# One core, a hybrid decoder block: keys replicated by transfers, output products halved, query rotation on GpSimd, and a re-ordered attention and tail

## What is computed

```python
xn = rms_norm(x, norm1_g)
u, q, k, v, qi, ki, wi, gs, ga = split(xn @ w_in)          # q, k, qi, ki get a rotary embedding
y_ssm = s5_mixer(u, ...)                                   # 32 groups of 64 complex states, a scan over the tokens
#   y = einsum(xr, c_re) - einsum(xi, c_im) + d * u ; gelu ; y * sigmoid(y @ w_glu + b_glu)
s = einsum('bthd,bsd->bths', qi, ki) * ID ** -0.5          # 16 index heads
score = einsum('bths,bth->bts', relu(s), wi)               # causal; the 64 best keys of each token are kept
p = softmax(q . k over the kept keys); y_att = p @ v       # 8 heads, 2 key heads
x = x + (sigmoid(gs) * (y_ssm @ w_proj_ssm) + sigmoid(ga) * (y_att @ w_proj_attn)) @ w_out
h = rms_norm(x, norm2_g)
gates = softmax over the 4 best of 32 of (h @ w_router)
for e in range(32):                                        # w_moe_in[e]: 1024 x 2048, w_moe_out[e]: 1024 x 1024
    z = h @ w_moe_in[e] + b_moe_in[e]
    out += gates[:, e] * (clamped_swiglu(z) @ w_moe_out[e] + b_moe_out[e])
return rms_norm(x + out, norm_f_g)
```

## Time and profile before

| | |
|---|---|
| Median of 3 runs | 1170.8 us (1169.01 to 1173.03) |
| The profiled execution | 1169.42 us, of which the span from first to last instruction is 1167.6 us |
| TensorE busy | 1118.3 us (96%) |
| VectorE busy | 343.2 us (29%) |
| ScalarE busy | 157.2 us (13%) |
| GpSimd busy | 0.7 us, seven memsets |
| Moved by DMA | 437.01 MB, mean 374 GB/s |

### The profile page before, as it was taken

One profiled execution on the slowest core, in us unless ns is written; L12 is line 12 of the kernel. 1 busy time (PEld: TensorE's weight loads), 2 busy tenths in 40 slices (PEclk: granted clock), 3 DMA queues, 4 the chain that ended last, 5 costly groups with the idle time before them and its releaser, 6 DMA issues.

```text
span 1167.6 us, 13800 instructions
## 1 busy us (share of the span) xinstructions
PE 1118.3 (96%) x5578; PEld 490.3 (42%) x5578; DVE 343.2 (29%) x760; ACT 157.2 (13%) x331; POOL 0.7 (0%) x7
## 2 busy tenths in 40 slices
PE   9999998989999999999999999999999999999995
PEld 8877786843333333333333333333333333333332
DVE  7999774221112221111111112211111111111112
ACT  2311433130001100010000001000000000000002
POOL 0000000000000000000000000000000000000000
PEclk9999998999999999999999999999999999999999
DMA  8343665589999999999999999999999999999992
GB/s 334 145 145 109 266 261 216 217 321 430 427 427 428 430 428 428 429 428 428 429 429 428 428 430 429 427 429 429 428 428 429 429 427 429 429 429 427 428 429 105
DMA packets 33434, 437.01 MB, mean 374 GB/s; under 512 B 3840, under 2 KB 3968, under 8 KB 5504
## 3 DMA queue, kind: packets, MB, share of 16 engines
q1 hardware_dynamic: 33120, 435.96, 89.1%
q10 hardware_dynamic: 288, 0.69, 0.2%
HBM read 435.58 MB, written 1.05 MB: 374 GB/s over the span
## 4 chain that ended last, share of the span: by engine, by line
PE 63%; DMA 22%; SPq 7%; DVE 6%; issue 1%; ACT 1%; DVEq 0%
PE ps L1277 25%; DMA mem<-in_w_moe 21%; PE ps L1325 13%; PE ps L1010 7%; SPq L359 7%; PE ps L1236 4%; PE ps L1253 3%; DVE mem L574 3%; PE ps L1211 2%; PE ps L1288 2%; PE ps L1188 1%; PE ps L1244 1%; PE ps L1310 1%; PE ps L1056 1%; PE ps L1107 1%
## 5 line engine op out<-in xcount | busy, mean ns | idle before, releaser
L1277 PE MATMUL ps<-mem,late 128*64 128x512 f32 x2048 | 458.2, 595 | 22.9 <-DMA mem<-in_w_moe 22.7
L1277 PEld LDWEIGHTS ps<-mem,late 128*64 128x64 f32 x2048 | 141.6, 137 | 330.7 <-issue 282.3
L1325 PE MATMUL ps<-mem,late 128*64 128x512 f32 x1024 | 226.8, 595 | 0.0
L938 DVE TENSOR_SCALAR late<-ps 128x512 f32<-128x512 f32 x32 | 22.1, 692 | 689.0 <-PE ps L1277 689.0
L1010 PE MATMUL ps<-mem 128*128 128x256 f32 x640 | 143.4, 382 | 0.0
L1010 PEld LDWEIGHTS ps<-mem 128*128 128x128 f32 x640 | 119.9, 190 | 21.0 <-issue 4.5
L1325 PEld LDWEIGHTS ps<-mem,late 128*64 128x64 f32 x1024 | 70.7, 137 | 133.3 <-issue 128.1
L537 ACT ACTIVATE late<-late 128x512 f32<-128x512 f32 x32 | 20.2, 630 | 514.9 <-DVE late L938 514.9
L1253 PE MATMUL ps<-late 64*128 64x512 f32 x256 | 63.6, 615 | 0.8 <-ACT late L544 0.8
L1236 PE MATMUL ps<-xs,late 128*64 128x512 f32 x256 | 63.5, 618 | 0.8 <-DVE late L574 0.8
L574 DVE TENSOR_TENSOR mem<-mem 128x1024 f32<-128x1024 f32 (+8 forms) x89 | 61.2, 729 | 6.5 <-ACT mem L429 3.7
(11 more groups left out here) (161 smaller groups left out, 518.9 us busy)
## 6 DMA issues: line engine op xcount, KB each, us to landing
mem<-in_w_moe SPq DMA_DIRECT2D x192, 2048.0 KB, 42.4
mem<-in_w_mix SPq DMA_DIRECT2D x26, 1024.0 KB, 5.4
mem<-in_w_mix SPq DMA_DIRECT2D x2, 512.0 KB, 7.3
out<-xs SPq DMA_DIRECT2D x2, 512.0 KB, 3.1
late<-in_turn_w SPq DMA_DIRECT2D x1, 640.0 KB, 3.9
late<-in_mix_tables SPq DMA_DIRECT2D x1, 576.0 KB, 14.8
mem<-in_x_t ACTq DMA_DIRECT2D x1, 512.0 KB, 4.6
mem<-in_x_t SPq DMA_DIRECT2D x1, 512.0 KB, 5.8
```

The source lines that it names most:

```text
L938: ve.tensor_scalar(gate_z, z[:, 0], LIMIT, None, ALU.min).then_inc(z_gate, 1)
L1277: i = pe.matmul(ps[r, n // 2, :], h_sel[:, k % 4, k // 4, :], w[:, 512 * n:512 * n + 512], start=(k == 0), stop=(k == KD - 1))
L1325: i = pe.matmul(ps[64 * q:64 * q + SLOTS, 2, :], act_tile(k), w[:, 512 * q:512 * q + 512], start=(k == 0), stop=(k == KF - 1))
```

## The change

1. **Output products.** VectorE subtracts and adds the four products in pairs, so that `y_out` has two products and two coefficient blocks (8 matmuls instead of 16).
2. **Query rotation.** The two `rope(qi_t)` go from VectorE to GpSimd, which starts as soon as QI0 and QI1 have been copied out.
3. **Keys by transfers.** The jobs KR0 to KR2 and their evictions go; SP copies the rotated keys with twelve transfers of 32 partitions.
4. **Order in the mixer stage.** The score jobs stand one x_job later (from the end of S3 to A1), `logits(0)` stands before A2 and `logits(1)` right after it, ahead of GLU; VectorE makes `y_raw` after `scores`; the choice for tile 1 is split; mask, exponentials, probabilities and attention of tile 1 run in two halves of four heads; `project` starts with the first half.
5. **Residual and bias.** The residual no longer goes through `diag`: the raw values are kept in `raw` and opened into the four banks by four matmuls with the identity (`open_sums`) in the routing stretch. The output bias goes into expert 1 as four matmuls on four row groups. Expert part 5 is issued after `opened` and `x_norm`, since `raw` lies there.
6. **The end.** `flag` is read in the second expert instead of after the last; ScalarE loads the Sqrt table before the end; the last norm goes tile by tile.

The diff, cut to its core:

```diff
-                for n, c in enumerate((0, 2, 1, 1)):
+                for n in range(2):
                     for a in range(4):
                         ins = pe.matmul(ps[32 * a:32 * a + 32, 2 + i // 2, (i % 2) * T:(i % 2) * T + T],
-                                        c_t[c][:, i, 32 * a:32 * a + 32], prod_out[n][:, a, :],
-                                        start=(n == 0), stop=(n == 3))
+                                        c_t[n][:, i, 32 * a:32 * a + 32], prod_out[2 * n][:, a, :],
+                                        start=(n == 0), stop=(n == 1))
...
-                tt(ct[2], tv[1], tv[0], ALU.subtract)
...
-                tt(prod_out[3], state_re, ei, ALU.mult).then_inc(out_ok, 1)
+                link(tt(prod_out[3], state_re, ei, ALU.mult))
+                tt(prod_out[0], prod_out[0], prod_out[1], ALU.subtract)
+                tt(prod_out[2], prod_out[2], prod_out[3], ALU.add).then_inc(out_ok, 1)
...
+            gp.wait_ge(consts_in, 16)
+            for n in range(2):
+                part = qi_t[:, 2 * n:2 * n + 2]
+                gp.wait_ge(*evicted(f"QI{2 * n}"))
+                gp.wait_ge(*evicted(f"QI{2 * n + 1}"))
+                if n:
+                    gp.wait_ge(queries_roped, 1)
+                gp.tensor_tensor(rope_c, part, cb, ALU.mult)
+                gp.tensor_tensor(rope_s, part, sn, ALU.mult).then_inc(rope_parts, 1)
+                gp.wait_ge(rope_parts, n + 1)
+                gp.tensor_tensor(part[:, :, 0, :], rope_c[:, :, 0, :], rope_s[:, :, 1, :], ALU.subtract)
+                gp.tensor_tensor(part[:, :, 1, :], rope_c[:, :, 1, :], rope_s[:, :, 0, :], ALU.add).then_inc(
+                    queries_roped, 1)
...
+            sp.wait_ge(roped, 1)
+            for n in (2, 0, 1):
+                for a in range(4):
+                    sp.dma_start(krep[32 * a:32 * a + 32, n], kk[32 * n:32 * n + 32]).then_inc(krep_in[n], 16)
+            load("A2")
...
-            x_job("S3", between=score_job)
-            x_job("A0", between=lambda step: score_job(4 + step))
+            x_job("S3", between=scores_from(-3))
+            x_job("A0", between=scores_from(1))
             y_out(3)
-            x_job("A1")
-            pe.wait_ge(tables_in, 16)
+            x_job("A1", between=scores_from(5))
+            logits(0)
             x_job("A2")
-            logits(0)
+            logits(1)
...
-            x_job("A3")
-            logits(1)
+            pe.wait_ge(tables_in, 16)
+            turn_prob(0)
+            x_job("A3")
...
-            sp.wait_ge(rstd_ok, 1)
+            sp.wait_ge(opened, 1)
+            sp.wait_ge(x_norm, TT)
             load_first(5)
...
-                        if adds:
-                            pe.wait_ge(diag_ok, 1)
...
-                body(first + 1, pairs, 1, opens=isinstance(c, int))
+                body(first + 1, pairs, 1, out_bias=isinstance(c, int))
+                if most_tokens:
+                    most_tokens()
```

More of the change, by code:

```diff
@@ L457, in _ @@
                 gate("S", gate_s, V_BG, n)
-            for n in range(3):
-                evict(f"KR{n}", krep[:, n], pair)
             def relus(*jobs):
@@ L542, in body @@
                                   ACT.Copy).then_inc(act_t_ok, 1)
+                    if tail:
+                        ready(ACT.Sqrt)
                     ac.wait_ge(chunk_used, j * NT + NT)
@@ L767, in scores, with choose_keys @@
                 ve.wait_ge(v_chain, chain[0])
-            def choose_keys(t):
+            def choose_keys(t, first, end):
                 w = P * (t + 1)
-                link(tt(score[:, t, 0:w], score[:, t, 0:w], causal[:, t, 0:w], ALU.add))
-                src = score[:, t, 0:w]
+                if first == 0:
+                    link(tt(score[:, t, 0:w], score[:, t, 0:w], causal[:, t, 0:w], ALU.add))
                 dst = taken[:, t, 0:w]
-                for n in range(NSEL // 8):
+                for n in range(first, end):
+                    src = dst if n else score[:, t, 0:w]
@@ L807, in _ @@
+            i.then_inc(y_raw_ok, 1)
+            choose_keys(0, 0, NSEL // 8)
+            mask(0, 0, NH)
+            choose_keys(1, 0, 5)
+            probabilities(0, 1, 0, NH)
+            choose_keys(1, 5, NSEL // 8)
             ve.wait_ge(*evicted("GLU1"))
@@ L809, in _ @@
             tt(y_ssm, y_gelu, glu_g, ALU.mult).then_inc(y_ssm_ok, 1)
-            choose_keys(1)
-            probabilities(0)
-            ve.wait_ge(*evicted("PS1"))
-            ve.wait_ge(*evicted("PS0"))
-            tt(p_ssm[:, 0:4, :], p_ssm[:, 0:4, :], gate_s[:, 0:4, :], ALU.mult)
-            mask(1)
+            for n in range(2):
+                mask(1, 4 * n, 4 * n + 4)
+            for n in range(2):
+                probabilities(1, 2 + n, 4 * n, 4 * n + 4)
             ve.wait_ge(rout_in, 16)
@@ L1085, in _ @@
             x_job("S2")
-            pe.wait_ge(roped, 1)
-            for n in range(3):
-                b = job(f"KR{n}")
-                r = slice(32 * n, 32 * n + 32)
-                for half in range(2):
-                    i = pe.matmul(b[:, half * T:half * T + T], sel[r, :], kk[r, half, :], start=True, stop=True)
-                i.then_inc(rot_done, 1)
             def score_job(n):
@@ L1216, in _, with open_sums @@
             aux(KD - 1)
+            def open_sums(t, q):
+                pe.wait_ge(tok_ok, 4 * q + 4)
+                return pe.matmul(ps[:, 4 + 2 * t + q, :], ident, raw[:, t, 512 * q:512 * q + 512], start=True,
+                                 stop=False, skip_group_check=True)
+            open_sums(0, 0)
+            open_sums(1, 0)
+            open_sums(0, 1)
             pe.wait_ge(picked_ok, 1)
@@ L1471, in packed_biases @@
     rows[:, 0:512] = b_in.reshape(NE, 4, 512).transpose(1, 0, 2).reshape(P, 512)
-    rows[0:2 * NE, 512:1024] = b_out.reshape(NE, 2, 512).transpose(1, 0, 2).reshape(2 * NE, 512)
+    rows[:, 512:1024] = np.tile(b_out.reshape(NE, 2, 512).transpose(1, 0, 2).reshape(2 * NE, 512), (2, 1))
     return rows
```

302 lines of the change are left out of this document (164 added, 138 removed).

## The result

The changed kernel took **1175.1 us** (median of 5 runs, 1173.74 to 1176.68), against 1170.8. The ratio is 1.0039, with a 95% interval of 1.0021 to 1.0058. So the kernel became slower by 4.3 us (the medians) to 4.6 us (the ratio), little more than the 3.5 us that can be told from no change. The prediction was 1173, in a range of 1162.5 to 1178. The profiled execution took 1175.11 us with a span of 1173.3 us; both are 5.7 us more than those of the profiled one of before.

The account below looks back on a forecast made before the run. Mixer stage and tail were taken to count in full around a weight-paced expert stream. The profiled 1169.4 - 6.7 (all but GpSimd) + 8.7 (GpSimd) = 1171.4, plus 1.4 to the median: 1172.8, say 1173 us; range 1162.5 to 1178.

Parts of the forecast that it names:

- the forecast's side: GpSimd and VectorE take turns at two-input work: delay 5.5 to 11.9 us, time 1169 to 1177, chance 0.47.
- the free case: Rival: GpSimd doesn't slow VectorE, whose operations of 1024 columns stay 1.16 us; 1164 us (1162 to 1167), chance 0.37.
- the held one: Rival: VectorE waits out each of GpSimd's eight operations in the mixer stage; 1177 to 1180 us, chance 0.12.
- What bounds the kernel: Whole run: mixer stage and tail count in full; between them 180 weight parts stream at 4.9 us each.
- Output products: Mixer stage: VectorE's added pairs make TensorE's third `y_out` wait some 4.5 us and start at 105.4, +5.1 us.
- Key transfers: Mixer stage: twelve transfers cost nothing, and the dropped key jobs save TensorE 2.9 us.
- Clock: TensorE: every idle stretch over 3.5 us costs a further 1.6 us through a slower granted clock.
- New order: Mixer stage: `logits(1)` waits 4.8 us plus 1.6 of slow clock, other waits go; W starts at 212.1, +1.5 us.
- routing: End of mixer stage: `open_sums` fill idle time and keep the clock up, `gates_turned` waits; -1.6 + 0.7 = -0.9 us.
- Tail: Experts 30 and 31: 7.8 us of matmuls go, transfers limit this to -5.9; `flag` read -1.0, norm -0.4.
- GpSimd beside VectorE: Mixer stage, rounds 1 and 2: GpSimd's query rotation delays VectorE, bounds 0 to 15.8 us, taken as +8.7.
- GpSimd holds VectorE whole: Rival: each of eight operations is waited out; first `y_out` waits over 14 us, third 17; 1177 to 1180, chance 0.12.

Follow-up runs that it names:

- the first experiment: The changed kernel without GpSimd's eight rotation operations, which only give their signals, so the index queries stay unrotated: 1163.53 us, ratio 0.9934.
- the experiment on the tail alone: The kernel before the change, without the diagonal matmuls of expert 30 and the output-bias matmuls of expert 31: 1164.02 us, ratio 0.9947.
- halves: The changed kernel with the query rotation cut into sixteen GpSimd instructions of half the length: 1174.72 us, ratio 1.0051.

## Why the prediction was right

The time lay in the range, on the forecast's side, and about 2 us above the point. That it lay in the range says little, since 1162.5 to 1178 took in most of the free case and the start of the held one. What was right is the account of the mixer stage, the stream and the tail; the term for GpSimd was too small, and its mechanism was nearer to the rival's. Step by step:

- **What bounds the kernel.** Right. The mixer stage counts in full (+13.4 at W, +12.1 at the first streamed transfer, +12.7 at the last part), the stream takes 4.9 us a part, and the tail counts.
- **Output products.** Right: +5.1 without GpSimd (third `y_out` at 105.4 in the first experiment). The wait before it was 3.45 us for the some 4.5 worked out, because TensorE came later itself after a slow clock behind the first `y_out`; in the kernel with the rotation under the PSUM reads, which had no slow clock there, it was 4.51. In the changed kernel it came at 118.0, not at 114.
- **Key transfers.** Right to cost them at nothing; they landed in 2.0 us each, and the worked-out start of W came out within 0.6 us in the kernel without GpSimd's work (212.7 for 212.1). The key jobs were not put back by themselves, so their -2.9 was measured only within that sum.
- **Clock.** Right in kind, but no fixed price fits. `logits(1)` took 3.57 us after an idle 4.50 us, and 2.01 us without one (the kernels with the copy-outs ahead), so 1.56 for the 1.6 taken. Other runs paid more behind the same wait: 2.6 us with the rotation back on VectorE (3.80 us, and 7.99 instead of 7.17 for the GLU jobs behind it). At the third `y_out` the 1.6 taken for an idle 4.5 us was 3.0 in the first experiment. And the bound of 3.5 us of idle time, below which no price was put, doesn't separate the cases: see the list at the end.
- **New order.** The wait before `logits(1)` was 4.50 (4.8 worked out). Mixer stage up to W +2.1 without GpSimd (+1.5); routing -1.3 (-0.9). Several scattered clock prices stand in this +2.1, so its nearness is partly luck.
- **Tail.** -5.8, and in the experiment on the tail alone -6.0 (-5.9). The `flag` read gave -0.4, inside its bounds of 0 to -2.3 but not the -1.0 taken. Norm -0.7 (-0.4).
- **GpSimd beside VectorE.** This is the term that was mis-sized. The sum took 8.7 us; VectorE was delayed by 12.6, beyond the 5.5 to 11.9 that bounded it, and the time rose by 11.1 to 11.6. Three choices in it were wrong. GpSimd's own time was taken as the middle of 7.3 and 15.8, and undisturbed it is 14.6; that the trace adds up to 15.8 just as the memsets gave is chance, since it includes GpSimd's own waiting. It was put at 54 us and started at 46.4, when QI0 and QI1 had been copied out. And the exemption of a quarter for PSUM reads didn't apply, since no such read of VectorE falls into the two bursts; there stand scans and short operations, nearly all with two inputs in SBUF. So VectorE lost 12.6 of 14.6 us, 0.86, and not three quarters. The sign that was named for the forecast, longer two-input operations of 1024 columns, didn't come: the six after the second burst take 7.03 us with and without GpSimd's work. It was shorter instructions that were held. The estimate by the pages of the Trainium skill, 13.8 us nearly all of it VectorE's delay, was nearer than the sum.

The rival "GpSimd holds VectorE whole" named the true mechanism, each of the eight instructions waited out, with a chance of 0.12 against the forecast's 0.47. It bounded the delay from below at 13 us, just above what came, and its price of 1177 was 2 us too high. The forecast and this rival differ little in kind: VectorE does get a turn after each GpSimd instruction, but only for one short instruction. In one sign both were wrong: the third `y_out` didn't wait 17 us, since TensorE had been held for 15.7 us at the first one already and waited 2.45 at the third.

With 12.6 in place of 8.7 the prediction's own sum for the profiled execution is 1175.3 us, and it took 1175.11. That this fits so closely is luck: between the profiled spans the rotation cost 11.1 us, and the rest of the change gave 5.4 and not 6.7.

The point from which the change is slower was given as a delay of 10.2 us, for slower by over 0.3%. With 12.6 the change is slower by 0.39%, and the interval of the ratio (1.0021 to 1.0058) reaches to both sides of that bound.

## What to carry to other kernels

Moving two-input work from VectorE to GpSimd is no relief while VectorE itself reads two inputs from SBUF: it costs VectorE nearly GpSimd's whole time, and that is about twice what VectorE would need. Put such work beside VectorE's reads of PSUM, or leave it on VectorE at a place where VectorE isn't late; the same rotation cost 11.6 us, nothing and 0.8 us in these three places, by the medians. And when a wait is moved on one engine, look at what stands behind the same signal on the others: here a copy-out behind the exponentials took the wait over twice, and only when both were moved ahead did it go.

## What the runs showed of the hardware

- A GpSimd operation with two inputs and one output took 2.35 to 2.38 us for 1024 columns and 1.26 to 1.31 for 512, when nothing held it; VectorE takes 1.16 for 1024. A memset of 1024 columns took 1.00 us.
- The holding is by whole instructions, and short ones suffer most: an operation of 128 columns took up to 2.43 us instead of 0.34. Scans, scalar-tensor-tensor operations and even an operation of 16 columns (1.18 us for 0.18) are held alike.
- GpSimd is held too (1.27 to 2.13 and 2.25 us), so its busy time in a contested stretch is not its own cost.
- What a slow clock costs behind an idle stretch of TensorE didn't go by the length of that stretch. The clock fell and cost 1.7 us behind an idle 2.45 us (changed kernel; 0.60 and 0.54 in the stretches behind it) and behind 1.83 us (fourth `y_out`, rotation back on VectorE; 0.71 and 0.50), and nothing behind 2.15 us (halves) and 2.12 us (third `y_out`, rotation back on VectorE). The same 3.45 us before the first `y_out` cost nothing with the rotation under the PSUM reads (1.07 us, and 4.19 for the job behind it, at a granted clock of 1.00), and 1.6 us without GpSimd's work (1.94 and 4.96, at 0.50). What decides between them isn't shown.
- GpSimd's memsets and VectorE's reads of PSUM are free of the holding: durations to within 0.01 us of those without. A TENSOR_SCALAR of 16 columns is the one exception found: 0.28 us beside a memset and 1.26 beside a GpSimd read, for 0.17.
